# Hymba encoder block on one core: a re-planned order of side work in eight-head attention, and the meta queries' scores by two products a piece in place of three

## What is computed

```
h = concatenate([meta, x])
q, k, v of 8 heads from low-rank projections; RMS norm; rope on 32 of 96 columns
y_mla = softmax(q k^T / sqrt(96)) v
y = concatenate([rmsnorm(y_lru), rmsnorm(y_mla)])
h = h + y @ w_out
h = h + (silu(dwconv(hn @ gate)) * (hn @ up)) @ w_down
return h[16:]
```

## Time and profile before

| what | value |
|---|---|
| median of the runs | 1302.21 us |
| the profiled execution's own time | 1303.02 us |
| its span | 1301.2 us |
| PE, DVE, ACT, POOL busy | 98%, 77%, 59%, 11% of the span |
| mean granted clock of PE | 0.993 of full speed |
| w_out loads (256 KB each), from issue to landing | 4.1 us median |

### The profile page before, as it was taken

The page is one execution under the profiler, slowest core; times in us unless marked ns, Lnnn a source line. Parts: engine busy times, 40 slices in busy tenths (PEclk is TensorE's granted clock), DMA queues, the critical chain, the costliest instruction groups (busy, mean ns, idle before and its releaser), DMA issues.

```text
span 1301.2 us, 18506 instructions
## 1 busy us (share of the span) xinstructions
PE 1271.2 (98%) x6158; PEld 1018.6 (78%) x6158; DVE 996.9 (77%) x1505; ACT 769.3 (59%) x1156; POOL 146.6 (11%) x175
## 2 busy tenths in 40 slices
PE   7999999899999999999999999999999999999998
PEld 7999997666666666687678888888888888888886
DVE  6677569678887876577779887887878887887855
ACT  7487648567765866534445565656474565656460
POOL 3000037400000001322200000000010000000010
PEclk9999999999999999999999999999999999999999
DMA  6111200000000014200144846576574847576667
GB/s 220 34 53 41 74 1 1 1 1 10 9 9 10 9 58 155 69 30 1 49 148 94 187 100 166 118 169 134 151 169 93 189 97 169 113 170 133 157 143 245
DMA packets 40938, 123.01 MB, mean 95 GB/s; under 512 B 7378, under 2 KB 8082, under 8 KB 34484
## 3 DMA queue, kind: packets, MB, share of 16 engines
q0 software_dynamic: 7200, 52.43, 21.4%
q1 hardware_dynamic: 33684, 69.86, 15.7%
HBM read 62.34 MB, written 59.80 MB: 94 GB/s over the span
## 4 chain that ended last, share of the span: by engine, by line
PE 85%; DVE 6%; ACT 5%; issue 2%; DMA 1%; POOL 0%; SPq 0%; DVEq 0%; ACTq 0%
PE banks L2911 30%; PE banks L2983 14%; PE banks L100 7%; PE banks L102 7%; PE banks L101 7%; PE banks L1935 2%; PE banks L2040 2%; PE banks L2041 2%; PE banks L2042 2%; PE banks L2060 2%; PE banks L2063 2%; PE banks L2061 2%; ACT e_f L1558 1%; PE banks L1895 1%; ACT e_h L1565 1%
## 5 line engine op out<-in xcount | busy, mean ns | idle before, releaser
L2911 PE MATMUL banks<-x_hi,slot_h 128*128 128x512 f32 x616 | 242.8, 394 | 2.5 <-DVE slot_l L2599 1.3
L2911 PE MATMUL banks<-x_lo,slot_h 128*128 128x512 f32 x616 | 243.4, 395 | 0.0
L2911 PE MATMUL banks<-x_hi,slot_l 128*128 128x512 f32 x616 | 242.9, 394 | 0.0
L2384 ACT ACTIVATE slot_h<-up_raw 128x512 fp32r<-128x512 f32 x127 | 79.8, 629 | 174.4 <-PE banks L2911 172.3
L2911 PEld LDWEIGHTS banks<-x_hi,slot_h 128*128 128x128 f32 x616 | 115.6, 188 | 30.9 <-DVE slot_l L2599 2.1
L2911 PEld LDWEIGHTS banks<-x_lo,slot_h 128*128 128x128 f32 x616 | 115.7, 188 | 27.1
L2911 PEld LDWEIGHTS banks<-x_hi,slot_l 128*128 128x128 f32 x616 | 115.7, 188 | 26.9
L2462 ACT ACTIVATE staged<-banks 128x1024 f32<-128x1024 f32 x100 | 101.4, 1026 | 41.0 <-PE banks L2983 41.0
L2983 PE MATMUL banks<-dn_h,a_h 128*128 128x512 f32 x280 | 110.4, 394 | 0.0
L2983 PE MATMUL banks<-dn_h,a_l 128*128 128x512 f32 x280 | 109.5, 391 | 0.0
L2983 PE MATMUL banks<-dn_l,a_h 128*128 128x512 f32 x280 | 109.5, 391 | 0.0
(11 more groups left out here) (346 smaller groups left out, 2861.5 us busy)
## 6 DMA issues: line engine op xcount, KB each, us to landing
down_sums<-staged POOLq DMA_DIRECT2D x50, 1024.0 KB, 8.0
up_raw<-in_w_up SPq DMA_DIRECT2D x88, 256.0 KB, 3.3
dn_raw<-in_w_down SPq DMA_DIRECT2D x22, 512.0 KB, 6.6
win_raw<-in_w_in SPq DMA_DIRECT2D x11, 512.0 KB, 3.3
x_tm<-in_x_tm SPq DMA_DIRECT2D x8, 512.0 KB, 6.0
wo_raw<-in_w_out SPq DMA_DIRECT2D x16, 256.0 KB, 4.1
h<-in_x_tm SPq DMA_DIRECT2D x8, 512.0 KB, 5.7
down_sums<-h SPq DMA_DIRECT2D x3, 1024.0 KB, 6.6
```

Of the source, the lines that this page charges most:

```text
L2384: nc.scalar.activation(s_h[slot], x, ACT.Copy).then_inc(sem["up_hi"], 1)
L2911: ins = nc.tensor.matmul(o, s[slot][:, k], xs[w], start=fresh and k == 0 and n == 0, stop=k == 3 and n == 2, skip_group_check=not fresh)
```

## The change

1. **Meta queries by two products.** tm writes the high parts of the last two meta queries to columns T-4 and T-3 of q_h, the low parts to T-2 and T-1. x0, x1, x2 multiply these four columns with k_h and with k_l: two products with four rows of output. ACT copies four rows; two DMAs per head move them to x_all and to a new x_low (x_in counts 32 a head), and head 7's turn on DVE adds x_low to x_all before the reduction.
2. **Their places.** Heads 1 to 6: x0 in slot 1, x1 in slot 2, x2 in slot 4. Head 7's: slots 5, 6 and 8 of head 6. Head 0's: slots 2, 4 and 5 of head 0.
3. **Head 0.** The transposes take the order tq0, tk0, tq1, tk1, wait for fewer tiles of the front, and use banks listed by hand (`side_banks`); a0 to a3 wait for two high parts only. `scores_ahead` computes the 12 main products of slots 0 and 1 without row 96 while the row's DMA flies, then adds row 96 by four products of one row. The warm-up products stand ahead of their jobs in other numbers (two for most, none behind am); `keep_busy` puts two products of the identity in each of the empty pv places of slots 0 and 1.
4. **Head 1's queries.** tq0 and tq1 of head 1 are in places 2 and 3 of slot 0, tk0 in place 3 of slot 1; both parts of these queries are made by DVE.
5. **SP.** The w_out loads move from the start of head 7's turn to behind `recip_row` in head 6's turn; the x rows of heads 0 to 6 move behind both.
6. **LRU tile 4 at the end.** Its products go ahead of the last pv (the meta keys of head 7). ACT splits LRU tile 6 before it reads the last output, tile 7 between w_out pieces; DVE adds tile 4 before it splits w_out 4 and 5, tile 5 before 6 and 7, tile 6 behind head 7's y_mla.

```diff
-    LAST_AHEAD.update({4: ("a5", "x0", "a6", "a7"), 5: ("a8", "x1", "a9", "a10"), 6: ("a11", "x2", "a12", "a13")})
-    FIRST = dict(PREPARE)
-    FIRST.update({8: ("x0", "x1", "x2", "")})
-    OWN = {1: ("", "", "x0", "x1"), 2: ("", "x2", "", "")}
+    LAST_AHEAD.update({5: ("a8", "x0", "a9", "a10"), 6: ("a11", "x1", "a12", "a13"), 8: ("x2", "", "", "")})
+    FIRST = {0: ("tq0", "tk0", "tq1", "tk1"), 1: ("a0", "a1", "a2", "a3"), 2: ("a4", "a5", "a6", "a7"),
+             3: ("tm", "a8", "a9", "a10"), 4: ("a11", "a12", "a13", "a14"), 5: ("a15", "am", "r", "")}
+    OWN = {1: ("", "", "x0", ""), 2: ("", "x1", "", ""), 4: ("", "x2", "", "")}
+    SECOND = dict(PREPARE)
+    SECOND.update({0: ("", "", "tq0", "tq1"), 1: ("", "", "", "tk0")})
+    OWN_FIRST = {2: ("", "x0", "", ""), 4: ("", "x1", "", ""), 5: ("", "x2", "", "")}
...
+    side_banks = [2, 3, 6, 7, 0, 1, 4, 5] + [(6, 7, 4, 5, 2, 3, 0, 1)[n % 8] for n in range(first - 9)] + [4] +\
+                 [6 + n % 2 for n in range(len(jobs) - first)]
...
-            if h == END:
-                sp.wait_ge(sem["ysum"], 4)
-                for k in range(4):
-                    sp.dma_start(raw_of(k), dram["w_out"][P * k:P * k + P, 0:half]).then_inc(sem["wo_a"][k], 16)
             def last_queries():
                 wait_read(sp, ("x2", h))
-                sp.dma_start(x_all[2 * h:2 * h + 2], x_one).then_inc(sem["x_in"], 16)
+                sp.dma_start(x_all[2 * h:2 * h + 2], x_one[0:2]).then_inc(sem["x_in"], 16)
+                sp.dma_start(x_low[2 * h:2 * h + 2], x_one[2:4]).then_inc(sem["x_in"], 16)

             if h == END:
                 last_queries()
             wait_read(sp, ("r", h))
             sp.dma_start(f32(q_h[h % 2][QK:QK + 1, 0:SEQ].rearrange("p (t n) -> p t n", n=P)), f32(r_row))\
               .then_inc(sem["row_in"], 16)
-            if h != END:
-                last_queries()
...
             if h:
                 recip_row(sp, h - 1)
+            if h == END - 1:
+                sp.wait_ge(sem["ysum"], 4)
+                for k in range(4):
+                    sp.dma_start(raw_of(k), dram["w_out"][P * k:P * k + P, 0:half]).then_inc(sem["wo_a"][k], 16)
+            if h != END:
+                last_queries()
...
-                        act.wait_ge(sem["x_in"], 16 * h)
+                        act.wait_ge(sem["x_in"], 32 * h)
...
             if h == HEADS and s == 2:
+                split_y("L", 6)
                 read_output(h)
...
             if (h, s) == (HEADS, 1):
+                add_lru(L_GAP)
                 split_w(4)
                 split_w(5)
-                add_lru(4)
...
+                if j in SPLIT_BY_DVE:
+                    link(nc.vector.tensor_scalar(hi[0:QK, cs], side[0:QK], gain[kind[1]], None, ALU.mult))
                 ins = low(lo[:, cs], side[0:QK], gain[kind[1]], hi[0:QK, cs])
...
+                link(nc.vector.tensor_tensor(x_all, x_all, x_low, ALU.add))
                 link(nc.vector.tensor_reduce(x_m, x_all, AX.X, ALU.max))
...
-        WARM = {"tk0": 10, "am": 8}
-        WARM.update({f"a{n}": 1 for n in range(2 * XT)})
+        WARM = {"tq0": 2, "tk0": 2, "tq1": 4, "tk1": 2, "a0": 6, "r": 2}
+        WARM.update({f"a{n}": 2 for n in range(2, 2 * XT)})
...
-                nc.tensor.matmul(side[0:2, 0:w], q_h[b][0:QK, qs], k_h[b][0:QK, ks], start=True, stop=False)
-                nc.tensor.matmul(side[0:2, 0:w], q_l[b][:, qs], k_h[b][0:QK, ks], start=False, stop=False)
-                ins = nc.tensor.matmul(side[0:2, 0:w], q_h[b][0:QK, qs], k_l[b][:, ks], start=False, stop=True)
+                q_parts = q_h[b][0:QK, T - 4:T]
+                nc.tensor.matmul(side[0:4, 0:w], q_parts, k_h[b][0:QK, ks], start=True, stop=False)
+                ins = nc.tensor.matmul(side[0:4, 0:w], q_parts, k_l[b][:, ks], start=False, stop=True)
...
+        def scores_ahead():
+
+            pe.wait_ge(sem["b_set"], 2 + len(LOWS))
+            for g in range(2):
+                ks = slice(P * g, P * g + P)
+                for c in range(2):
+                    cs = slice(512 * c, 512 * c + 512)
+                    out = s_ps(g)[:, cs]
+                    nc.tensor.matmul(out, k_h[0][0:QK, ks], q_h[0][0:QK, cs], start=True, stop=False)
+                    nc.tensor.matmul(out, k_h[0][0:QK, ks], q_l[0][:, cs], start=False, stop=False)
+                    nc.tensor.matmul(out, k_l[0][:, ks], q_h[0][0:QK, cs], start=False, stop=False)
+            pe.wait_ge(sem["row_in"], 16)
+            for g in range(2):
+                for c in range(2):
+                    cs = slice(512 * c, 512 * c + 512)
+                    ins = nc.tensor.matmul(s_ps(g)[:, cs], k_h[0][QK:QK + 1, P * g:P * g + P], q_h[0][QK:QK + 1, cs],
+                                           start=False, stop=True)
+                ins.then_inc(sem["s_done"], 1)
...
+            if g - 2 == G - 1:
+                for k in range(LF):
+                    lru_products(L_GAP, k)
             for c in range(2):
                 if 0 <= g - 2 < G:
                     pv(g - 2, c)
+                elif 0 <= g < 2:
+                    keep_busy(2)
```

More of the change, by code:

```diff
@@ L1091, in side_jobs @@
         places = [None] * 4
-        ahead = FIRST if h < 0 else LAST_AHEAD if h == END - 1 else PREPARE
-        for plan, head in [(ahead, h + 1), (META_QUERIES, h), (LRU_SUMS, h), (OWN, h)]:
-            if plan is OWN and not 1 <= h < END:
+        ahead = FIRST if h < 0 else SECOND if h == 0 else LAST_AHEAD if h == END - 1 else PREPARE
+        own = OWN if h else OWN_FIRST
+        for plan, head in [(ahead, h + 1), (META_QUERIES, h), (LRU_SUMS, h), (own, h)]:
+            if plan is own and not 0 <= h < END:
                 continue
@@ L1118, in side_of @@
     def side_of(j):
[L1120 to L1123, removed]
+        return bank(side_banks[number[j]], 1)
     def before(j):
         n = number[j]
[L1128 to L1132, removed]
+        return [i for i in jobs[:n] if side_banks[number[i]] == side_banks[n]][-1:]
+    SPLIT_BY_DVE = [("tq0", 1), ("tq1", 1)]
+    FIRST_KEYS = [("a0", 0), ("a1", 0), ("a2", 0), ("a3", 0)]
     def hi_upto(j):
-        return sum(HIGH.get(i[0], 0) for i in jobs[:number[j]])
+        return 2 if j in FIRST_KEYS else sum(HIGH.get(i[0], 0) for i in jobs[:number[j]] if i not in SPLIT_BY_DVE)
     def wait_read(eng, j):
@@ L1910, in job @@
                 wait_read(pe, i)
-            if number[j] < 6 or j == ("tm", 0):
-                done = {"tq0": 8, "tq1": 8, "tk0": 8, "tk1": 8}.get(kind, NT)
-                pe.wait_ge(sem["q_scaled"], done)
-                pe.wait_ge(sem["kv_read"], done)
-                pe.wait_ge(sem["rope_done"], done)
-                pe.wait_ge(sem["v_full"], done)
+            if number[j] < 8 or j == ("tm", 0):
+                for name, done in zip(("q_scaled", "kv_read", "rope_done", "v_full"), HEAD_0.get(kind, (NT,) * 4)):
+                    if done:
+                        pe.wait_ge(sem[name], done)
+            if h == 0 and kind in WARM:
+                for _ in range(WARM[kind]):
+                    nc.tensor.matmul(side[:, 0:P], ident, ident, start=True, stop=True)
             if kind[:2] in ("tq", "tk"):
@@ L1965, in job @@
             ins.then_inc(sem["side_done"], 1)
-            if h == 0 and kind in WARM:
-                if kind == "a0":
-                    pe.wait_ge(sem["kv_read"], NT)
-                for _ in range(WARM[kind]):
-                    nc.tensor.matmul(bank(3 if kind == "tk0" else 5)[:, 0:P], ident, ident, start=True, stop=True)
         def meta_pv(s, i):
@@ L2044, in scores, with keep_busy @@
                 ins.then_inc(sem["s_done"], 1)
+        def scores_ahead():
[15 more added lines that the diff above has]
+                ins.then_inc(sem["s_done"], 1)
+        def keep_busy(n):
+            for _ in range(n):
+                nc.tensor.matmul(bank(5)[:, 0:P], ident, ident, start=True, stop=True)
         def pv(g, c):
@@ L2078, in tensor @@
                     pv(g - 2, c)
+                elif 0 <= g < 2:
+                    keep_busy(2)
                 place_job(h, s, js, 2 + c)
-        for j in range(4, XT):
+        for j in range(L_GAP + 1, XT):
             for k in range(LF):
```

45 lines of the change are left out of this document (28 added, 17 removed).

## The result

The changed kernel takes **1307.27 us** (median of 8 runs, 1304.37 to 1309.26), the kernel before 1300.8 (median of 8): ratio 1.0052, 95% interval 1.0042 to 1.0062. That is 6.5 us slower. (Ratios go by fast runs alone, so single runs of 7115 us, of the kernel before, and of 2523 us, of addition early, are not in them.) The forecast of 1302.0 and "no change" was wrong in sign: the losses beat the gains, by more than the interval leaves open, if by far less than 2%. The profiled execution has a span of 1306.9 us where 1301.2 was before.

The account below looks back on a forecast made before the run. PE was taken as the bound, busy for 98% of the span. Gains of 9.35 us and losses of 9.2 against the profiled 1303.02 or the median 1302.21 gave 1302.9 or 1302.1; forecast 1302.0 us, no change, range 1293 to 1310.

Parts of the forecast that it names:

- item 5: Head 6, before a10: PE waits for x rows that SP sends behind the w_out loads; 5.1 us lost (4.0 to 6.5).
- item 6: PE behind head 6's wait: lower clock for nine products; 1.7 us lost (0 to 3.4).
- 1.0 and 0.75 of products and places: Gains predicted for head 6's new places (1.0 us) and for head 7's x0 to x2 with a gap gone (0.75).
- Item 2: Heads 1 to 6: new places of x0 to x2 and a product less shorten PE's waits; 4.3 us gained (2.9 to 6.5).
- third rival: Removed products don't count, PE waits at x1 and a0 anyway, item 2 vanishes: 1306.4 us; chance 0.1.
- item 1: Attention, each head: two products in place of three for x0 to x2 save PE 0.49 us a head.
- Item 7: Head 7: later r row (1.2) and DVE's x_low addition (1.2); 2.4 us lost (1.0 to 3.2).
- Items 4 and 8: Head 0's preparation brings scores earlier, 1.3 us gained; LRU tile 4 fills PE's gap at attention's end, 3.0 gained.
- slower: the clock: PE from slot 6 of head 6 on: each new standstill brings a lower-clock stretch, 4.7 us more, 1306.8; chance 0.2.

Follow-up runs that it names:

- addition early: Kernel of r row first, with DVE's addition of the low rows at the start of slot 1 of head 7, ahead of e_l: 1297.80 us, ratio 0.9995.
- third product: Kernel of addition on POOL, with the second product of each piece of the meta queries' scores made twice: 1295.70 us, ratio 0.9964.
- old places: Kernel of addition on POOL, with x0 to x2 and SP's order as before the change in heads 1 to 5: 1296.14 us, ratio 0.9976.
- Gap open: Kernel of addition on POOL, with LRU tile 4 back behind the last pv: 1298.20 us, ratio 0.9993.
- queries as before: Changed kernel with the meta queries' part undone: three products, old places, old SP order, no low rows or addition: 1297.27 us, ratio 0.9972.
- r row first: Kernel of x rows first, with head 7's r row sent ahead of its two x rows: 1296.39 us, ratio 0.9979.
- x rows first: Changed kernel, with SP in head 6 sending the x rows ahead of the reciprocal row and w_out loads: 1298.83 us, ratio 0.9987.
- filled wait: Changed kernel, with 26 unread products of the identity on PE before a10 of head 7: 1304.15 us, ratio 1.0022.
- x rows before loads: Changed kernel, with SP in head 6 sending the x rows behind the reciprocal row but ahead of the w_out loads: 1301.81 us, ratio 1.0020.
- mixed places: Changed kernel with new places in heads 1 to 5 only; heads 6 and 7 have old places and SP order: 1296.97 us, ratio 0.9970.
- addition on POOL: Kernel of mixed places, with the addition of the low rows on POOL in place of DVE: 1295.11 us, ratio 0.9963.

## Why the prediction was wrong, by its own steps

Items 2 to 8 are in the trace with the signs that they were given; the sum of -0.15 us failed by 5.6 against the +5.45 of the trace up to the feed-forward part. The step that failed above all is the flight in item 5. These terms were mis-sized:

- **Item 5, the new wait in head 6** (5.1, in fact 6.74) and **item 6, the clock after it** (1.7, in fact 2.8). The step of item 5 that failed is "the second lands 2.3 us later, as the r row of 484.46 did by 486.76". PE reached a10 2.1 us ahead of x_low's sending (471.07 and 473.16), as predicted (474.45 and 476.65); but that r row had flown alone. Behind the loads the flight is 4.0 us, and with the x rows ahead of the loads 2.45. Item 5's own bound for this case, 6.5 "if they land with the w_out data", was the right case. The Trainium skill (DMA: Bandwidth & Descriptors, Queues, rings and completion order), which the prediction set beside its sum, says that descriptors on a DMA engine are taken in ring order; the trace agrees, with the rows' packets at 476.13 to 476.49 and the last of the loads' at 476.25. (The 4.1 us beside that sentence in the prediction are of the profile's page.) Item 6 took nine products from the old stretch; a standstill 2.5 times as long was followed by 14. From r 6 to r 7 the prediction has 5.1 + 1.7 less 1.0 and 0.75 of products and places, 5.05; it was 8.18. This is 3.1 of the 5.6.
- **Item 2, heads 1 to 5** (3.3 of its 4.3, in fact 2.0; third rival): in heads 2 to 4 I took 0.5 each, they gave 0.17, 0.19 and 0.26. PE still waits for DVE's tk1 at a0 (0.56 in head 2) and now for ACT at x1 (0.30). The third rival was half right. The removed products, item 1's "0.49 us a head", are worth that in head 0 and next to nothing in heads 1 to 4: eight cost 0.10 us there (third product), and by old places -0.06. But item 2 does not vanish with them, since the places gain by themselves. 1.3 of the 5.6.
- **Item 7, head 7** (2.4, in fact 3.8): the r row (1.5 for 1.2) and the addition (0.6 more by the start of L100, for 1.2) come to 2.2 for 2.4 together. Missing was the low clock behind the longer wait at L100, 8 products at 0.2 more each. 1.4 of the 5.6.
- **Items 4 and 8** gave 1.6 and 3.8 for 1.3 and 3.0. Gap open and queries as before show that they are gains of their own. Together 1.1 us more than predicted, which the sum has to subtract.
- The front, which has no edit, took 0.85 longer in this execution, and what lies behind y_h 0.1.

The rival "slower: the clock" named 1306.8 and came nearest, in part by luck: 2.7 of its 4.7 us more were clock (1.1 in head 6, 1.6 in head 7), and the rest of the miss was the flight and the places. It was right in the mechanism, two stretches of low clock; its places were half right, since the second came behind the addition and not before head 7's first scores, and head 0's preparation gained its full part.

The sum had seven terms that cancelled to 0.15 us. A forecast of "no change" from gains and losses of 9 us each was the weakest reading of such a sum: half of the loss hung on one chain of transfers, and no row of before showed their flight in the new order. Nor is it so that a change of under 2% can't be told from none here: the interval of the ratio is 0.1% either way.

## What to carry to other kernels

When a small DMA is moved past bulk loads on its queue, size its flight as the loads' landing and not as the flight of a lone small one, and send first what an engine in order will wait for. Take a product off a bound engine only where no wait of that engine follows for another one: here, in heads 1 to 4, a third product was worth nearly nothing and the place of the job 0.36 us a head. A short operation added for it belongs on the engine that has idle time, by its timeline in those very slots, even if it takes twice as long there; that shows in the trace here, and less in the timed runs.

## What the runs showed of the hardware

- The low clock does not follow the length of a standstill alone. It came behind 6.74 and 3.15 us in head 6, behind 2.73 at the end of attention (before and gap open), and behind a wait of 1.64 (r row first); it did not come behind 1.99 (x rows first), 2.16 (addition early) and the last 2.80 of the filled wait, which short products preceded. The same 1.67 us before L100 was followed by it in five executions (changed, x rows first, x rows before loads, filled wait, mixed places) and not in a sixth (r row first). For waits of about 2 us it is a chance, not a term of fixed size; in these places it costs 1.6 to 2.8 us when it comes.
- It also comes with PE busy throughout: in head 5, behind 1.97 us of two-column products, in ten of fourteen profiles and not in the other four. There it costs 0.5 us (gap open against addition on POOL); where it lasted twice as long (third product), head 5 is 3.5 longer than without it.
- Two rows of 8 KB sent behind 1 MB of loads on SP's queue move as the loads end, 4.0 us from the second's sending to its use; sent ahead of them, 2.45 us.
- An addition of 16 x 1040 takes 1.24 us on DVE and 2.41 on POOL.
